# A softmax's reciprocal put first and its band product last in each DVE step, and the convolution's squares added earlier on POOL

## The chip, the cores and the metric

The kernel runs on one core of a Trainium2 chip. Its engines work in parallel, each through its own list of instructions in order, and meet at semaphores: TensorE (PE in the profile) multiplies matrices, VectorE (DVE) and ScalarE (ACT) work on vectors, GpSimd (POOL) too, and SyncE (SP) issues most DMAs. The metric is the device time of one execution in microseconds.

## The reference

A first transformer block is followed by two equal layers (sizes: 512 positions, width 1024, 16 query heads of 64 in 2 groups). The change lies in the two layers, in their attention and in the convolution beside it:

```python
# attention: each query block of 128 sees its own block and the one before, and a "sink"
s = jnp.einsum('bnqkgd,bnskd->bnkgqs', qb, kb) * scale
s = jnp.where(mask[None, :, None, None], s, -jnp.inf)
m = jnp.maximum(jnp.max(s, axis=-1, keepdims=True), sink)
p = jnp.exp(s - m)
p = p / (jnp.sum(p, axis=-1, keepdims=True) + jnp.exp(sink - m))
o = jnp.einsum('bnkgqs,bnskd->bnqkgd', p.astype(v.dtype), vb)
# convolution of 31 taps over the positions, then a layer norm over 512 channels
a = u * jax.nn.sigmoid(ug)
y = conv(a, w_dw) + b_dw
y = jax.nn.silu(layernorm(y, ln_g, ln_b))
c_out = jnp.einsum('btc,cd->btd', y, w_pw)
merged = jax.nn.sigmoid(ga) * a_out + jax.nn.sigmoid(gb) * c_out
x = x + jnp.einsum('btd,de->bte', merged, w_out[l])
```

## The kernel before

All large products are made in fp32 as three TensorE passes over split operands (L418, L419, L420: high by high, low by high, high by low), 512 columns each. Weights stream in units; ScalarE takes the high part, DVE the low part of each.

The attention of a layer is cut into 32 jobs (`LJ`), each a pair of heads on one block of 128 queries. A loop of 36 steps t is written out in the list of every engine, and the lists meet at semaphores (`A[...]`), which count jobs. What a job j passes through, and on which engine:

- TensorE, step j: scores, `scores` (L2140).
- DVE, step j, in `softmax`: a masked copy that packs the two key blocks into one (L2425; not in the last 8 jobs, of the first block), then for each head a custom instruction that adds the mask, scales and takes the maximum (L2441).
- ScalarE, step j: the exponential and its sum (L2287).
- DVE, step j+1, in `softmax`: the reciprocal of the sums (L2429).
- POOL, step j+1: the product with it, `scaled` (L2630), after a copy of the sink column for the job of that step (L2624).
- TensorE, step j+3: the transpose of the probabilities, `turn` (L2148). It writes a bank that the band product of the job before must have read: it waits for `A["banded"]` of job j-1.
- DVE, step j+3: the band product, `banded` (L2454), which puts the transposed probabilities apart for the two key blocks.
- TensorE, step j+4: the product with the values, `values` (L2161). DVE, step j+4: the gating, `gated` (L2463).

Between `turn` and `values` TensorE fills each step with chunks of other products, three passes each: the gates, and then the convolution's output product. How many is in the table `FILL_AT` (steps 4, 8, 11 and 13 have none, most have one to six). DVE has more work behind the gating in many steps: the gates' evictions (L2499, L2471), halves of weight splits (L796, L800), and the convolution's layer norm.

The layer norm's variance is made in the loop: DVE takes the mean off in steps 3 and 4, ScalarE squares, POOL adds the four squares to one in `sums_of_squares` (L2644), and TensorE sums over channels at the end of step 7 (`AT_SS`, L336). ScalarE takes the root (L2308), DVE inverts it in step 9 (L2517), and TensorE spreads it in step 13 (L343).

Of the kernel before, what the change touches and what calls it, by code (L numbers as in the profile page):

```python
# [101 lines left out]
def build(nc, w, x, mem, pos, pack, tables, cmask, w2, wg, rope2, out):  # L102
    ctx = ExitStack()
    with ctx:
        def sem(name):
            return ctx.enter_context(nc.semaphore(name))
# [1753 lines left out]
        def cross_dve(dve):  # L1860
# [92 lines left out]
            for j in range(11):  # L1953
# [14 lines left out]
        A = {n: sem("a_" + n) for n in ("scores", "packed", "max", "exp", "rec", "scaled", "turned",  # L1968
                                        "banded", "pv", "gated")}
        sink_in = sem("a_sink_in")  # L1970
        LJ = QB * 8
# [28 lines left out]
        def prob_at(j):  # L2000

            return j % 4

        def score_bank(j):

            return 2 if j % 2 == 0 else 0
# [5 lines left out]
        def block_of(j):  # L2012

            return (j // 8 + 1) % QB

        def query_factor(j, e=None):

            c = (j % 8 * QB + block_of(j)) * 2
            return rcol_head[:, c:c + 2] if e is None else rcol_head[:, c + e:c + e + 1]
# [4 lines left out]
        def asm(j, a_, e=None):  # L2024
            c = 16 * (j % 4) + a_
            return small[:, c:c + 2] if e is None else small[:, c + e:c + e + 1]
# [313 lines left out]
        def layer_dve(dve, L):  # L2340
# [76 lines left out]
            def softmax(j, o):  # L2417

                j, o = j if j < LJ else None, o if 0 <= o < LJ else None
                first = j is not None and block_of(j) == 0  # L2420
                if j is not None and not first:

                    pair = bank[:, score_bank(j):score_bank(j) + 2, :]
                    dve.wait_ge(A["scores"], (L * LJ + j + 1) * 2)
                    dve.copy_predicated(pair[:, :, P:2 * P], mask_b[:, P:2 * P].bitcast(U16).unsqueeze(1).to_broadcast([P, 2, P]),  # L2425
                                        pair[:, :, 0:P]).then_inc(A["packed"], 1)
                if o is not None:
                    dve.wait_ge(A["exp"], (L * LJ + o + 1) * 2)
                    dve.reciprocal(asm(o, 12), asm(o, 4)).then_inc(A["rec"], 1)  # L2429
                if j is not None:  # L2430
                    if j == 0:
                        dve.wait_ge(q_inv, L * 2 + 2)
                    if j >= 4:
                        dve.wait_ge(A["turned"], L * LJ + j - 3)
                    if not first:
                        dve.wait_ge(A["packed"], L * 24 + j + 1)
                    for e in range(2):
                        c = 2 * (j % 8) + e
                        if first:
                            dve.wait_ge(A["scores"], (L * LJ + j) * 2 + e + 1)  # L2440
                        dve.tensor_tensor_reduce(lprob[:, prob_at(j), e, 0:P], bank[:, score_bank(j) + e, P:2 * P],  # L2441
                                                 mask_b[:, P:2 * P] if first else mask_b[:, 0:P],
                                                 query_factor(j, e), neg_sink[:, L, c:c + 1], ALU.add, ALU.min, asm(j, 0, e)).then_inc(A["max"], 1)
# [34 lines left out]

            taps(FIRST_TAPS)
            for t in range(STEPS):  # L2480
                if 0 <= t - LAG_T < LJ:
                    banded(t - LAG_T)
                softmax(t, t - 1)
                if 0 <= t - LAG_V < LJ:
                    gated(t - LAG_V)
                if t == STEPS - 1:
                    dve.wait_ge(A["gated"], L * LJ + LJ)
                    dve.wait_ge(mg_sum, L * 8 + 7)
                    dve.wait_ge(co_ready, L * 8 + 8)
                    dve.tensor_tensor(sgb[:, 7, :], sgb[:, 7, :], sga[:, 7, :], ALU.add).then_inc(mg_sum, 1)  # L2490
                if t == 2:
                    roped(4)
                for f in FILL_END.get(t, ()):
                    if f < 6:
                        if f % 2:
                            dve.wait_ge(unit_done, L * V_N + base + V_FILL + f // 2 + 1)
                        else:
                            dve.wait_ge(fill_half, L * 3 + 6 + f // 2 + 1)
                        dve.tensor_tensor(sgb[:, 2 + f, :], bank[:, FILL_BANK[f], :], rbc[:, :], ALU.mult).then_inc(l_gs, 1)  # L2499
                    else:  # L2500
                        conv_gated(f - 6)
                if MERGE_LO_AT <= t:
                    merged_lo(t - MERGE_LO_AT)
                if t - 1 in L_SPLIT_AT:
                    n, p = L_SPLIT_AT[t - 1]
                    split_lo_part(dve, Unit(base + n, L), p, L * 6 + 6 + n - 16)
                if t < len(JOB_TAPS):
                    taps(JOB_TAPS[t])
                if t == AT_MEAN:
                    dve.wait_ge(ln_sum, L + 1)  # L2510
                    dve.tensor_scalar(acc[:, :], bank[:, 5, :], 1.0 / 512, None, ALU.mult).then_inc(ln_mu, 1)
                for m in CENTRE_AT.get(t, ()):
                    dve.wait_ge(ln_mu, L + 1)
                    dve.tensor_tensor(cy[:, m, :], cy[:, m, :], acc[:, :], ALU.subtract).then_inc(ln_c, 1)
                if t == AT_INV:
                    dve.wait_ge(cstd_ready, L + 1)
                    dve.reciprocal(rcol_ln[:, :], rcol_ln[:, :]).then_inc(cinv_ready, 1)  # L2517
                for m in NORM_AT.get(t, ()):
                    dve.wait_ge(crow_done, L + 2)
                    dve.wait_ge(ln_c, L * 4 + m + 1)  # L2520
                    dve.tensor_tensor(cy[:, m, :], cy[:, m, :], bank[:, 5, :], ALU.mult).then_inc(ln_n, 1)
                for m in LO_AT.get(t, ()):
                    dve.wait_ge(ln_hi, L * 4 + m + 1)
                    dve.tensor_tensor(c_lo[:, m, :], cy[:, m, :], c_hi[:, m, :], ALU.subtract).then_inc(ln_lo, 1)
# [61 lines left out]
        def _(pool):  # L2586
# [39 lines left out]
            def scaled(L, j):  # L2626
                row = lprob[:, prob_at(j), :, 0:P]
                pool.wait_ge(A["exp"], (L * LJ + j + 1) * 2)
                pool.wait_ge(A["rec"], L * LJ + j + 1)
                pool.tensor_tensor(row, row, asm(j, 12).unsqueeze(2).to_broadcast([P, 2, P]), ALU.mult).then_inc(A["scaled"], 1)  # L2630
# [6 lines left out]
            def sums_of_squares(L, which):  # L2637

                for n in which:
                    a_, b_ = ((0, 1), (2, 3), (0, 2))[n]  # L2640
                    pool.wait_ge(ln_sq, L * 4 + max(a_, b_) + 1)
                    if n == 2:
                        pool.wait_ge(ln_add, L * 3 + 2)
                    pool.tensor_tensor(conv_squares(a_), conv_squares(a_), conv_squares(b_), ALU.add).then_inc(ln_add, 1)  # L2644

            for L in range(LAYERS):
                pool.wait_ge(unit_done, L * V_N + U_L)
                pool.tensor_tensor(la[:, :, 0:PAD], ones_pad, ones_pad, ALU.subtract).then_inc(pad_ready, 1)
                pool.wait_ge(ident_in, TABLES_BEFORE + L * 16 + 16)
                for t in range(9):  # L2650
                    if t == 0:
                        pool.wait_ge(q_n, L + 1)
                    if t == 1:
                        pool.wait_ge(q_tabs, L * 2 + 1)
                    if t >= 2:
                        pool.wait_ge(q_rope, L * 9 + t - 1)
                    pool.tensor_tensor(lcos[:, t % 2, 0:T], lq[:, rope_at(t), :], cos_q[:, :] if t else cos2, ALU.mult).then_inc(q_cos, 1)
                for t in range(STEPS):
                    if t == 0:
                        pool.wait_ge(setup_step, SINKS_NEGATED)  # L2660
                        pool.wait_ge(q_ss, L * 9 + 9)
                    if t < LJ:
                        sink_column(L, t)
                    if t in (6, 7):
                        sums_of_squares(L, (0,) if t == 6 else (1, 2))
                    if 0 <= t - 1 < LJ:
                        scaled(L, t - 1)
                    if MERGE_HI_AT <= t:
                        merged(L, t - MERGE_HI_AT)
                for n in (1, 2) if L + 1 < LAYERS else (1,):  # L2670
                    sum_squares(pool, L * 2 + NORM_L + n)
# [125 lines left out]
```

## Time and profile before

| | us |
|---|---|
| three runs | 2242.09, 2242.54 (median), 2244.86 |
| profiled execution | 2238.4 |
| its span, first to last instruction | 2236.5 |
| TensorE busy | 2210.1 |
| DVE busy | 1284.1 |
| the loops, layer 0 and layer 1 | about 1026 to 1152 and 1716 to 1842 |

TensorE is almost never idle over the whole span, while DVE is busy for 57% of it. In the first part of each loop, though, DVE is busy nearly all the time. A row of the timeline gives start, length, engine, line, operation, output and inputs, the count of equal instructions merged, and in brackets the idle time of the engine before it with what ended it. DVE's instructions overlap: the next one starts some 0.1 us before the last has ended, so the time that one takes in a row of them is read from start to start.

### The profile page before, as it was taken

Reading aid. Unit: us, or ns where it says so; the run is one execution under the profiler, and the core shown is the slowest. Engines: PE = TensorE matmul, PEld = TensorE weight load, DVE = VectorE, ACT = ScalarE, POOL = GpSimd, SP = SyncE. Lnnn points to the kernel's source line nnn. Section 1 sums busy time; section 2 is a strip of 40 time slices with the busy share of each in tenths; the row PEclk is TensorE's granted clock in tenths of the full one; section 3 lists DMA queues with packets and bytes.
Section 4 is the critical chain, followed back from the end, with each engine's and each line's share of the span. In section 5 each row is a group of like instructions: output and inputs, shape, how many; then the busy total and the mean of one; then the engine's idle time right before and its main releaser. Section 6 shows DMA issues by size and latency. Waiting matters only on the chain.

```text
span 2236.5 us, 28991 instructions
## 1 busy us (share of the span) xinstructions
PE 2210.1 (99%) x11244; PEld 1805.3 (81%) x11244; DVE 1284.1 (57%) x1956; ACT 846.0 (38%) x1299; POOL 259.3 (12%) x281
## 2 busy tenths in 40 slices
PE   9999999999999999999999999999999999999999
PEld 7887788898888898886678888888887668888887
DVE  6468656445444226999874444332889874544422
ACT  5545454354333225223544333222322633433311
POOL 3000032120000001022231000011003232000000
PEclk9999999999999999999999999999999999999999
DMA  6221033123222222221122222223321122322222
GB/s 221 103 76 57 20 120 126 57 76 113 94 94 94 104 103 83 102 76 57 57 76 94 94 94 100 106 96 108 109 79 57 39 76 76 119 104 97 94 104 84
DMA packets 30484, 203.44 MB, mean 91 GB/s; under 512 B 3504, under 2 KB 4144, under 8 KB 6704
## 3 DMA queue, kind: packets, MB, share of 16 engines
q1 hardware_dynamic: 29088, 197.34, 24.7%
q10 hardware_dynamic: 1296, 4.72, 0.6%
q8 instruction: 68, 1.11, 0.2%
q14 instruction: 32, 0.26, 0.0%
HBM read 199.95 MB, written 2.10 MB: 90 GB/s over the span
## 4 chain that ended last, share of the span: by engine, by line
PE 87%; DVE 9%; issue 2%; ACT 1%; POOL 1%; DMA 0%; ACTq 0%; DVEq 0%; POOLq 0%
PE bank L418 25%; PE bank L420 25%; PE bank L419 25%; DVE cy L2361 3%; PE bank L2161 1%; PE bank L1005 1%; PE bank L2140 1%; DVE w_lo L304 1%; PE bank L2148 1%; PE bank L976 1%; POOL acc L327 1%; PE bank L2040 1%; PE bank L993 1%; DVE bank L2374 1%; PE bank L518 1%
## 5 line engine op out<-in xcount | busy, mean ns | idle before, releaser
L418 PE MATMUL bank<-x_hi,w_hi 128*128 128x512 f32 (+1 forms) x2032 | 789.9, 389 | 5.5 <-DVE x_lo L1777 2.3
L420 PE MATMUL bank<-x_hi,w_lo 128*128 128x512 f32 (+1 forms) x2032 | 775.0, 381 | 0.0
L419 PE MATMUL bank<-x_lo,w_hi 128*128 128x512 f32 (+1 forms) x2032 | 774.1, 381 | 0.0
L304 DVE TENSOR_TENSOR w_lo<-w_raw,w_hi 128x2048 fp32r<-128x2048 f32 x167 | 386.3, 2313 | 408.8 <-ACT w_hi L300 408.8
L300 ACT ACTIVATE w_hi<-w_raw 128x2048 fp32r<-128x2048 f32 x167 | 319.7, 1916 | 586.9 <-PE bank L420 585.0
L418 PEld LDWEIGHTS bank<-x_hi,w_hi 128*128 128x128 f32 x2032 | 382.1, 188 | 83.7 <-issue 6.6
L420 PEld LDWEIGHTS bank<-x_hi,w_lo 128*128 128x128 f32 x2032 | 381.9, 188 | 74.4
L419 PEld LDWEIGHTS bank<-x_lo,w_hi 128*128 128x128 f32 x2032 | 382.5, 188 | 72.7 <-issue 2.9
L418 PE MATMUL bank<-f_hi,w_hi 128*128 128x512 f32 (+1 forms) x572 | 213.3, 373 | 0.0
L419 PE MATMUL bank<-f_lo,w_hi 128*128 128x512 f32 (+1 forms) x572 | 213.2, 373 | 0.0
L420 PE MATMUL bank<-f_hi,w_lo 128*128 128x512 f32 (+1 forms) x572 | 213.2, 373 | 0.0
L2361 DVE SCALAR_TENSOR_TENSOR cy<-la,gains,cy 128x512 f32<-128x512 f32 x240 | 173.1, 797 | 0.0
L566 DVE TENSOR_TENSOR bank<-bank,rbc 128x512 f32<-128x512 f32 x66 | 46.0, 697 | 167.6 <-PE bank L420 159.6
L418 PEld LDWEIGHTS bank<-f_hi,w_hi 128*128 128x128 f32 x572 | 107.7, 188 | 19.1
L420 PEld LDWEIGHTS bank<-f_hi,w_lo 128*128 128x128 f32 x572 | 107.7, 188 | 19.0
L419 PEld LDWEIGHTS bank<-f_lo,w_hi 128*128 128x128 f32 x572 | 107.7, 188 | 18.6
L327 POOL TENSOR_TENSOR acc<-acc,sq 128x512 f32<-128x512 f32 (+1 forms) x48 | 80.6, 1680 | 142.0 <-ACT sq L311 138.3
L2287 ACT ACTIVATE lprob<-lprob,small 128x129 f32<-128x129 f32 x128 | 50.5, 396 | 101.9 <-DVE small L2441 101.9
L555 ACT ACTIVATE f_hi<-bank 128x512 f32 x66 | 39.5, 598 | 114.5 <-DVE bank L572 114.5
L574 DVE TENSOR_TENSOR f_lo<-bank,f_hi 128x512 f32 x66 | 45.7, 692 | 58.4 <-ACT f_hi L555 58.4
L327 POOL TENSOR_TENSOR acc<-sq 128x512 f32<-128x512 f32 (+1 forms) x8 | 14.4, 1800 | 442.8 <-ACT sq L311 442.8
L553 ACT ACTIVATE silu<-bank 128x512 f32<-128x512 f32 x66 | 38.8, 588 | 54.7 <-DVE bank L566 54.5
(360 smaller groups left out, 2624.0 us busy)
## 6 DMA issues: line engine op xcount, KB each, us to landing
w_raw<-w_d SPq DMA_DIRECT2D x184, 1024.0 KB, 4.8
out_d<-h SPq DMA_DIRECT2D x8, 256.0 KB, 6.5
h<-x_d ACTq DMA_DIRECT2D x3, 512.0 KB, 9.3
tab<-rope_d ACTq DMA_DIRECT2D x2, 768.0 KB, 4.2
memT<-mem_d ACTq DMA_DIRECT2D x1, 1024.0 KB, 4.8
w_raw<-w_d SPq DMA_DIRECT2D x2, 256.0 KB, 4.2
h<-x_d ACTq DMA_DIRECT2D x2, 256.0 KB, 5.9
w_raw<-w_d SPq DMA_DIRECT2D x1, 512.0 KB, 6.6
```

What stands on the lines that cost most here:

```text
L300: act.activation(w_hi[:, u.slot, :], w_raw[:, u.slot, :], ACT.Copy).then_inc(hi_ready, 1)
L304: dve.tensor_tensor(w_lo[:, u.slot, :], w_raw[:, u.slot, :], w_hi[:, u.slot, :], ALU.subtract).then_inc(lo_ready, 1)
L327: pool.tensor_tensor(acc[:, 0:width], sq[:, 0, 0:width] if k == 1 else acc[:, 0:width], sq[:, k % 2, 0:width], ALU.add).then_inc(acc_ready, 1)
L418: pe.matmul(dst, wh[:, k, cols], hi[:, kx_, at:at + width], start=start, stop=False)
L419: pe.matmul(dst, wh[:, k, cols], lo[:, kx_, at:at + width], start=False, stop=False)
L420: return pe.matmul(dst, wl[:, k, cols], hi[:, kx_, at:at + width], start=False, stop=stop)
L553: act.activation(silu[:, :], g, ACT.Silu).then_inc(silu_done, 1)
L555: act.activation(pick(f_hi, j, i), up, ACT.Copy).then_inc(f_hi_done, 1)
L566: dve.tensor_tensor(g, g, rbc[:, :], ALU.mult).then_inc(gu_scaled, 1)
L574: dve.tensor_tensor(pick(f_lo, j, i), up, pick(f_hi, j, i), ALU.subtract).then_inc(f_lo_done, 1)
L2287: act.activation(row, row, ACT.Exp, bias=asm(j, 0, e), scale=-1.0, accum_out=asm(j, 4, e)).then_inc(A["exp"], 1)
L2361: dve.scalar_tensor_tensor(out=cy[:, m, :], in0=src, scalar=wt, in1=cy[:, m, :], op0=ALU.mult, op1=ALU.add).then_inc(l_tap, 1)
```

## The change

DVE's `softmax` issues the reciprocal of the job before first, ahead of the masked copy of the new job, and the loop calls `softmax` ahead of `banded`. POOL adds the convolution's squares in steps 5 and 6 instead of 6 and 7, and behind `scaled` instead of ahead of it.

```diff
                 first = j is not None and block_of(j) == 0
+                if o is not None:
+                    dve.wait_ge(A["exp"], (L * LJ + o + 1) * 2)
+                    dve.reciprocal(asm(o, 12), asm(o, 4)).then_inc(A["rec"], 1)
                 if j is not None and not first:
                     pair = bank[:, score_bank(j):score_bank(j) + 2, :]
                     dve.wait_ge(A["scores"], (L * LJ + j + 1) * 2)
                     dve.copy_predicated(...).then_inc(A["packed"], 1)
-                if o is not None:
-                    dve.wait_ge(A["exp"], (L * LJ + o + 1) * 2)
-                    dve.reciprocal(asm(o, 12), asm(o, 4)).then_inc(A["rec"], 1)
...
             for t in range(STEPS):
+                softmax(t, t - 1)
                 if 0 <= t - LAG_T < LJ:
                     banded(t - LAG_T)
-                softmax(t, t - 1)
                 if 0 <= t - LAG_V < LJ:
                     gated(t - LAG_V)
...
                     if t < LJ:
                         sink_column(L, t)
-                    if t in (6, 7):
-                        sums_of_squares(L, (0,) if t == 6 else (1, 2))
                     if 0 <= t - 1 < LJ:
                         scaled(L, t - 1)
+                    if t in (5, 6):
+                        sums_of_squares(L, (0,) if t == 5 else (1, 2))
```

DVE's list of step 4 in layer 0 before (`lband` is the band product's output, `small` holds a job's maxima, sums and reciprocals, `lprob` its probabilities, `sga` its gated output):

```order
L2454 TENSOR_TENSOR lband<-bank,tab_133 128x512
L2425 COPY_PREDICATED bank<-mask_b,bank 128x2x128
L2429 RECIPROCAL small<-small 128x2
L2441 ISA lprob,small<-bank,mask_b,neg_sink,rcol_head 128x128
L2441 ISA small 128x1
L2441 ISA lprob,small<-bank,mask_b,neg_sink,rcol_head 128x128
L2441 ISA small 128x1
L2463 SCALAR_TENSOR_TENSOR sga<-sga,bank 128x128
L796 TENSOR_TENSOR w_lo<-w_raw,w_hi 128x1024
```

The same step in the changed kernel, with the head of step 5 behind it:

```order
L2423 RECIPROCAL small<-small 128x2
L2428 COPY_PREDICATED bank<-mask_b,bank 128x2x128
L2441 ISA lprob,small<-bank,mask_b,neg_sink,rcol_head 128x128
L2441 ISA small 128x1
L2441 ISA lprob,small<-bank,mask_b,neg_sink,rcol_head 128x128
L2441 ISA small 128x1
L2454 TENSOR_TENSOR lband<-bank,tab_133 128x512
L2463 SCALAR_TENSOR_TENSOR sga<-sga,bank 128x128
L796 TENSOR_TENSOR w_lo<-w_raw,w_hi 128x1024
L2514 TENSOR_TENSOR cy<-cy,acc 128x512 x2
L2423 RECIPROCAL small<-small 128x2
```

The reciprocal is the first instruction of the step, the band product stands behind the two maxima and ahead of the gating, and the reciprocal of the next step follows the layer norm's part. (The line numbers of the two moved instructions of `softmax` differ: 2423 and 2428 for 2429 and 2425.)

POOL's list in steps 5 to 7 of layer 0, as a difference:

```order
 L2630 TENSOR_TENSOR lprob<-lprob,small 128x2x128
+L2644 TENSOR_TENSOR la<-la 128x512
 L2624 COPY lprob<-neg_sink 128x2
-L2644 TENSOR_TENSOR la<-la 128x512
 L2630 TENSOR_TENSOR lprob<-lprob,small 128x2x128
+L2644 TENSOR_TENSOR la<-la 128x512 x2
 L2624 COPY lprob<-neg_sink 128x2
-L2644 TENSOR_TENSOR la<-la 128x512 x2
```

Each addition of squares (`la`) stands ahead of a sink copy that it stood behind, and behind the same product `scaled` (L2630) as before. The lists of TensorE, ScalarE and SyncE are the same.

## Rows read from the trace of the kernel before

**Rows 1.** The page's totals, TensorE's part of the line.
```profile
PE 2210.1 (99%) x11244; PEld 1805.3 (81%) x11244; DVE 1284.1 (57%) x1956; ACT 846.0 (38%) x1299; POOL 259.3 (12%) x281
```
**Rows 2.** TensorE's waits: total us, times, longest.
```profile
PE bank L336 <- POOL la L2644: 3.5, 2, 1.7
...
PE bank L2148 <- DVE lband L2454: 3.0, 4, 1.1
```
**Rows 3.** Timeline, layer 0, steps 6 and 7: POOL's additions, TensorE's sums behind them.
```profile
1053.54 3.31 POOL L2644 TENSOR_TENSOR la<-la 128x512 f32<-128x512 f32 x2
...
1056.89 1.05 PE L336 MATMUL bank<-ones,la 128*128 128x1 f32 x8 [1.73 <-POOL la L2644]
```
**Rows 4.** Timeline, layer 0, DVE in step 4.
```profile
1043.22 0.69 DVE L2454 TENSOR_TENSOR lband<-bank,tab 128x512 f32<-128x512 f32 x1
...
1043.82 0.42 DVE L2425 COPY_PREDICATED bank<-mask_b,bank 128x256 f32<-128x256 uint16 x1
...
1044.15 0.16 DVE L2429 RECIPROCAL small<-small 128x2 f32<-128x2 f32 x1
...
1044.39 0.41 DVE L2441 CUSTOM_DVE_ANT_0 lprob<-bank,mask_b,neg_sink 128x128 f32<-128x128 f32 x1
...
1045.06 0.29 DVE L2463 SCALAR_TENSOR_TENSOR sga<-sga,bank 128x128 f32<-128x128 f32 x1
```
**Rows 5.** Timeline, layer 0, DVE in steps 0 and 1.
```profile
1030.62 0.42 DVE L2425 COPY_PREDICATED bank<-mask_b,bank 128x256 f32<-128x256 uint16 x1
...
1031.20 0.41 DVE L2441 CUSTOM_DVE_ANT_0 lprob<-bank,mask_b,neg_sink 128x128 f32<-128x128 f32 x1 [0.15 <-DVE bank L2425]
...
1034.19 0.17 DVE L2429 RECIPROCAL small<-small 128x2 f32<-128x2 f32 x1
...
1034.32 0.41 DVE L2441 CUSTOM_DVE_ANT_0 lprob<-bank,mask_b,neg_sink 128x128 f32<-128x128 f32 x1
```
**Rows 6.** Timeline, layer 0, TensorE's transpose in step 5.
```profile
1044.05 0.41 PE L2148 MATMUL bank<-ident,lprob 128*128 128x128 f32 x2 [1.08 <-DVE lband L2454]
```
**Rows 7.** Timeline, layer 0, steps 8 to 12: DVE, and TensorE's transpose of step 12.
```profile
1059.67 0.69 DVE L2454 TENSOR_TENSOR lband<-bank,tab 128x512 f32<-128x512 f32 x1 [1.32 <-PE bank L2148]
...
1063.55 0.17 DVE L2429 RECIPROCAL small<-small 128x2 f32<-128x2 f32 x1 [0.42 <-ACT lprob L2287]
...
1064.76 0.29 DVE L2463 SCALAR_TENSOR_TENSOR sga<-sga,bank 128x128 f32<-128x128 f32 x1 [0.34 <-PE bank L2161]
...
1066.24 0.66 DVE L2454 TENSOR_TENSOR lband<-bank,tab 128x512 f32<-128x512 f32 x1
...
1069.85 0.44 PE L2148 MATMUL bank<-ident,lprob 128*128 128x128 f32 x2
```
**Rows 8.** Timeline, layer 0: DVE's steps 13, 19, 23, and the transposes one step later.
```profile
1074.00 0.69 DVE L2454 TENSOR_TENSOR lband<-bank,tab 128x512 f32<-128x512 f32 x1
...
1075.55 0.44 PE L2148 MATMUL bank<-ident,lprob 128*128 128x128 f32 x2
...
1100.09 0.69 DVE L2454 TENSOR_TENSOR lband<-bank,tab 128x512 f32<-128x512 f32 x1
...
1101.65 0.44 PE L2148 MATMUL bank<-ident,lprob 128*128 128x128 f32 x2
...
1111.93 0.69 DVE L2454 TENSOR_TENSOR lband<-bank,tab 128x512 f32<-128x512 f32 x1
...
1113.35 0.44 PE L2148 MATMUL bank<-ident,lprob 128*128 128x128 f32 x2
```
**Rows 9.** Timeline, layer 1: TensorE's transposes of steps 5 and 14.
```profile
1734.73 0.41 PE L2148 MATMUL bank<-ident,lprob 128*128 128x128 f32 x2 [1.08 <-DVE lband L2454]
...
1765.38 0.44 PE L2148 MATMUL bank<-ident,lprob 128*128 128x128 f32 x2
```
**Rows 10.** Stretches of 5 us: busy us of each engine, then granted clock, DMA share, GB/s.
```profile
1057.00:1062.00 5.00, 5.00 (x29) 3.17 (x30) 3.39 (x14) 3.09 (x7) 1.35 (x4) 0.66 0.01 3
1748.00:1753.00 5.00, 5.00 (x35) 3.54 (x34) 4.01 (x14) 4.07 (x9) 1.02 (x4) 1.00 0.02 3
```

## The prediction, made before the changed kernel was run

> **What bounds the kernel now.** I read the page's totals first, then TensorE's list of waits, then the timeline of the two attention loops (steps 0 to 35 of each layer). TensorE is busy in 99% of the span [rows 1], so only what makes TensorE stand still, or run at half clock, can move the time. Its waits that this change can touch are few: twice 1.7 us for POOL's sums of squares, and 3.0 us in four pieces, 1.1 the longest, for DVE's band product [rows 2]. The first is what the POOL part aims at; the second is a wait that the DVE part can lengthen. TensorE hardly waits in the loop because DVE delivers the band product early in each step, so I asked how much earlier than needed.
>
> **The change, part by part.** Nothing is added or removed; a DVE step and two places in POOL's list are put in another order.
>
> *POOL.* The squares move from step 6 to 5 and from 7 to 6, but also behind `scaled`. In POOL's list they therefore pass one sink copy and nothing else: each addition still follows the same `scaled`, which waits for the same reciprocal. The two late additions took 3.31 us and ended at 1056.85; TensorE's sums of squares waited 1.73 us for them [rows 3]. By itself the POOL part is worth the one copy at each place, a few tenths at most, and nothing below that bound except the sink copy behind 3.3 us of additions; the exponential that needs it comes later still. I take 0.
>
> *DVE: the length of a step.* Before, step 4 runs: band product at 1043.22, masked copy 0.60 later, reciprocal, first maximum at 1044.39, gating at 1045.06: 1.84 us [rows 4]. The reciprocal stood in the pause that the first maximum has behind the masked copy: with it there the maximum starts 0.57 after the copy [rows 4], without it 0.58 [rows 5]. So taking it out of there saves nothing, and in front it costs its own slot, 0.13 [rows 5]. A step grows to 1.97. In steps 1 to 3, which have one wait less in front of the maximum, reciprocal and copy together took 0.33 + 0.13 = 0.46 and will take 0.13 + 0.58 = 0.71: 0.25 each, 0.75 together.
>
> *DVE: the band product.* TensorE's transpose of job t-2 in step t+1 may start only when DVE's step t has done the band product of job t-3. That now starts 0.13 + 0.58 + 0.67 = 1.38 after DVE's step begins and takes 0.69; the transpose started 0.14 after it ended (1043.91, 1044.05) [rows 4, 6]. So the transpose is freed 2.21 us after DVE's step begins, where it was 0.83. Not shown in this trace is whether the maximum can start sooner when no reciprocal was just issued: its two bounds are 0.46 and 0.58, taken as 0.58 as in the only row of that kind. With 0.46 the 2.21 is 2.09. Now along the loop, where "late" is against layer 0 of the trace:
>
> - Step 4: DVE starts it at 1043.22 + 0.75 = 1043.97; the transpose that ran at 1044.05 runs at 1046.18, 2.13 late. Behind it in TensorE's queue stands everything: fill products, values, scores.
> - Step 7: TensorE reached the sums of squares at 1056.89 - 1.73 = 1055.16 and will reach them at 1055.16 + 2.2 = 1057.4, after POOL's 1056.9. The POOL wait is gone, eaten by the new one: 0.5 late.
> - Step 8: DVE comes 0.75 + 4 x 0.13 = 1.3 late, but had stood 1.32 for a transpose that waited behind those sums [rows 7]. The band product being last, that wait goes, and DVE starts step 8 as before, 1059.67. The reciprocal of job 8 came 3.88 later, at 1063.55, having waited for ScalarE, which waits for the maximum. The maximum now starts at 0.71 instead of 1.17, so the reciprocal comes at 1063.1, and now heads step 9.
> - Steps 9 to 11: step 9 is 1.97 plus what stood behind its gating (1064.76 to 1066.24, 1.48) [rows 7]: step 10 starts at 1066.55. Step 10 is 1.97 + 0.2 for gating: step 11 starts at 1068.7. Its band product frees the transpose of step 12 at 1070.9; it ran at 1069.85 [rows 7]: 1.05 late.
> - Step 13: DVE waits in step 12 for TensorE's values, so it comes equally late, 1074.00 + 1.05 = 1075.05; the transpose is freed at 1077.26 instead of 1075.55 [rows 8]: 1.7 late.
> - Steps 14 to 35: with three fill chunks or more in a step TensorE does not notice. Where the next step has one or two and DVE has a weight split or a gate behind its gating, it does: step 19 began at 1100.09 and frees at 1102.30 what ran at 1101.65, 0.65; step 23 at 1111.93 frees at 1114.14 what ran at 1113.35, 0.79, of which 0.25 are covered because DVE is by then less late than TensorE [rows 8]. There are five such places (16, 19, 20, 22, 23), about 2.1 us together, an estimate from these two and from the same subtraction at the others. After step 24 the masked copy falls away and the margin returns; at step 32 both wait for DVE's last gate, which is as late as TensorE.
>
> So 1.7 + 2.1 = 3.8 us in layer 0. In layer 1 the same step 13 came 0.85 us sooner relative to step 4 (1765.38 - 1734.73 against 1075.55 - 1044.05) [rows 8, 6, 9], because TensorE lost clock in layer 0 only: 0.66 granted in 1057 to 1062, 1.00 at the same place of layer 1 [rows 10]. The new path is set by DVE in both, so layer 1 loses 4.65. Sum 8.4 us: the profiled execution of 2238.4 (span 2236.5) would become 2246.8. The median of the runs shown, 2242.54, lies 4.1 above it; I carry the 8.4 over: **2250.9 us**. With 2.09 in place of 2.21 in the seven waits of a layer the sum is some 1.6 smaller: 2249.3.
>
> **The clock.** TensorE idles 1.73 us at the sums of squares in both layers; afterwards layer 0 ran at 0.66 of full clock, 1.2 and 2.4 GHz mixed, layer 1 at 1.00, which is 2.4 GHz [rows 3, 10]; so such a wait sometimes costs the full level. The Trainium skill (TensorE: Matmul & The Clock Gate, What's actually happening) says that half rate is the default and activity releases it, which speaks against a change that opens a longer idle stretch. The trace agrees in layer 0 and not in layer 1; by that rule the new stretch in step 5 would cost each layer what the second rival below gives.
>
> **The rivals.**
> 1. *Hidden after step 13.* The five late waits don't come, because DVE runs further ahead once it no longer waits for a transpose at the head of a step (TensorE's only long waits now stand in steps 5 and 7). Left is 1.7 + 2.55 = 4.2: 2246.7, within no change. Against it: at step 19 the margin was 0.73 and the delay is 1.38.
> 2. *Half clock at the new wait.* In step 5 TensorE stands from about 1043.9 to 1046.2, longer than the 1.73 that lost the clock in one layer of two. A stretch like that of rows 10 costs 5.00 x (1 - 0.66) = 1.7 us; in both layers 3.4 on top: 2254.3.
> 3. *Faster.* The reciprocal in front lets POOL scale and add sooner, the two POOL waits go (2 x 1.73) with layer 0's lost 0.85, and the band product is still in time: 2242.5 - 4.3 = 2238.2. It decides at step 5: if the band product of step 4 ends by the end of TensorE's scores, near 1043, this is what comes. For it speaks that the POOL wait is the longest touched; against it that DVE was already 1.08 us too late at just that place with the band product first [rows 6].
> 4. *The POOL part does nothing.* Its list passes only a copy; that is in the forecast and costs it nothing.
>
> **How the numbers follow.** Forecast 0.52, rival 2 0.22, rival 1 0.17, rival 3 0.09. A measurement of this kernel tells changes above 0.2%, 4.5 us, from none; slower by more than that are the forecast and rival 2, 0.74, within it rival 1, 0.17, faster rival 3, 0.09. The range reaches from 2243.5, which leaves out rival 3 and part of rival 1, to 2256, rival 2 with 1.7 us for a masked copy or weight split that collides with POOL's additions. The forecast's own range is 2248 to 2253.
>
> **What would show it.** TensorE's wait for the band product grows from 3.0 to 10 us or more, about 3 at step 5 of each layer, and appears at steps 12, 14, 20, 21 and 24; the wait for POOL's additions is gone; DVE's reciprocal opens each step, and DVE waits for ScalarE at step 9 longer than 0.42. It is wrong if the band product still ends before the scores of the next step, if steps 17 to 24 show no new wait, or if the sums of squares still wait for POOL.

## The result, and the profile after

The changed kernel takes 2244.86 us (median of 20 runs, 2243.05 to 2247.12), the kernel before 2241.45 us beside it (20 runs, 2238.77 to 2244.86). The ratio is 1.0015, 95% interval 1.0009 to 1.0021: 3.4 us slower. Slower was forecast, and 2244.86 lies in the range, but the forecast was 2250.9 and its step 8.4 us; less than half of that came. One run of experiment 6 below took 2635.81 us, at a mean granted clock of 0.781, and is left out of its numbers.

The profiled execution of the changed kernel took 2244.4 us, its span 2242.5, against 2238.4 and 2236.5: profile against profile it is 6.0 us. First the totals and TensorE's list of waits (total us, times, longest), which answer to [rows 1, 2]:

```profile
PE 2211.9 (99%) x11244; PEld 1806.2 (81%) x11244; DVE 1280.9 (57%) x1956; ACT 846.6 (38%) x1299; POOL 257.8 (11%) x281
```

```profile
PE bank L2148 <- DVE lband L2454: 11.2, 14, 2.2
PE bank L418 <- DVE w_lo L304: 2.7, 2, 1.6
...
PE bank L418 <- issue: 0.7, 2, 0.3
```

The wait for POOL's additions (3.5 us) is gone, and the wait for the band product has grown from 3.0 to 11.2 us, as forecast. Two lines were not foreseen: the wait at L418, TensorE's wait for the last gate in step 32, fell from 2.1 to 0.7, and a wait for a weight split (`w_lo`, L304) grew from 2.0 to 2.7, at 23 us into the run, where no instruction was moved. The first scores of layer 0 come 0.72 later than before (1027.48 for 1026.76), about as much as that wait has grown, so times within a loop are compared below from its first scores.

The timeline of step 4 and of the head of step 5, layer 0, after; it answers to [rows 4, 6]:

```profile
1043.93 0.16 DVE L2423 RECIPROCAL small<-small 128x2 f32<-128x2 f32 x1
1044.00 0.41 DVE L2428 COPY_PREDICATED bank<-mask_b,bank 128x256 f32<-128x256 uint16 x1
...
1044.56 0.41 DVE L2441 CUSTOM_DVE_ANT_0 lprob<-bank,mask_b,neg_sink 128x128 f32<-128x128 f32 x1
...
1045.22 0.69 DVE L2454 TENSOR_TENSOR lband<-bank,tab 128x512 f32<-128x512 f32 x1
...
1046.06 0.62 PE L2148 MATMUL bank<-ident,lprob 128*128 128x128 f32 x2 [2.19 <-DVE lband L2454]
1046.33 0.78 PE L418 MATMUL bank<-x_hi,w_hi 128*128 128x512 f32 x1
...
1049.97 0.39 PE L418 MATMUL bank<-x_hi,w_hi 128*128 128x512 f32 x1
```

The transpose starts 2.13 after DVE's step (2.21 was worked out): the reciprocal in front costs 0.07 from start to start, not 0.13. Behind the 2.19 us of standing still the fill products take 0.62 to 0.78 us each instead of 0.39; the first that takes 0.39 again starts at 1049.97. POOL, and the sums that wait for it, after [rows 3]:

```profile
1054.26 2.52 POOL L2644 TENSOR_TENSOR la<-la 128x512 f32<-128x512 f32 x2
...
1055.99 1.86 DVE L796 TENSOR_TENSOR w_lo<-w_raw,w_hi 128x1024 fp32r<-128x1024 f32 x1
...
1058.65 1.05 PE L336 MATMUL bank<-ones,la 128*128 128x1 f32 x8
```

The additions end at 1056.78, for 1056.85 before. From the first scores they start at the same place (26.78 us) and end 0.8 sooner, because they take 2.52 us instead of 3.31: DVE's weight split, which lay beside both of them, now starts during the second. The sums come 1.04 later than before by the same count and wait for nothing. The rest of the loop, by the transposes of layer 0 in steps 9, 12, 14, 20, 21 and 24, and the last gate in step 32 [rows 7, 8]:

```profile
1062.95 0.41 PE L2148 MATMUL bank<-ident,lprob 128*128 128x128 f32 x2 [1.03 <-DVE lband L2454]
...
1071.79 0.41 PE L2148 MATMUL bank<-ident,lprob 128*128 128x128 f32 x2 [0.55 <-DVE lband L2454]
...
1077.83 0.41 PE L2148 MATMUL bank<-ident,lprob 128*128 128x128 f32 x2 [0.32 <-DVE lband L2454]
...
1104.47 0.41 PE L2148 MATMUL bank<-ident,lprob 128*128 128x128 f32 x2 [0.50 <-DVE lband L2454]
...
1108.30 0.41 PE L2148 MATMUL bank<-ident,lprob 128*128 128x128 f32 x2
...
1116.89 0.41 PE L2148 MATMUL bank<-ident,lprob 128*128 128x128 f32 x2 [0.41 <-DVE lband L2454]
...
1138.58 0.41 PE L2148 MATMUL bank<-ident,lprob 128*128 128x128 f32 x2 [0.80 <-DVE lband L2454]
...
1139.33 0.47 PE L418 MATMUL bank<-o_hi,w_hi 128*128 128x512 f32 x1 [0.34 <-issue]
```

The same stretch of step 32 in the kernel before:

```profile
1134.67 0.41 PE L2148 MATMUL bank<-ident,lprob 128*128 128x128 f32 x2 [0.40 <-DVE lband L2454]
...
1136.14 0.47 PE L418 MATMUL bank<-o_hi,w_hi 128*128 128x512 f32 x1 [1.06 <-issue]
```

From its first scores (L2140) to DVE's last merge (L2490) the loop took 121.11 us in layer 0 and 120.20 in layer 1 before, 123.55 and 123.03 after: 2.44 and 2.83 more, 5.27 of the 6.0; the other 0.7 is the later start of the first loop. These loop lengths are the measure used below.

### The profile page after: what moved, and what is told of

It is laid out like the page before. It is cut to its first block, busy times and chain, and to the rows that moved or that the text cites. A ratio compares the mean times of both kernels' runs of the same rounds, so it can differ in the third digit from the quotient of the medians.

```text
span 2242.5 us, 28991 instructions
## 1 busy us (share of the span) xinstructions
PE 2211.9 (99%) x11244; PEld 1806.2 (81%) x11244; DVE 1280.9 (57%) x1956; ACT 846.6 (38%) x1299; POOL 257.8 (11%) x281
## 4 chain that ended last, share of the span: by engine, by line
PE 86%; DVE 10%; issue 2%; ACT 1%; POOL 1%; DMA 0%; ACTq 0%; DVEq 0%; POOLq 0%
PE bank L418 25%; PE bank L420 25%; PE bank L419 25%; DVE cy L2361 3%; PE bank L1005 1%; PE bank L2161 1%; DVE w_lo L304 1%; PE bank L2148 1%; PE bank L976 1%; POOL acc L327 1%; PE bank L2140 1%; PE bank L2040 1%; PE bank L993 1%; DVE lprob L2441 1%; DVE bank L2374 1%
## 5 line engine op out<-in xcount | busy, mean ns | idle before, releaser
L418 PE MATMUL bank<-x_hi,w_hi 128*128 128x512 f32 (+1 forms) x2032 | 791.5, 390 | 6.4 <-DVE w_lo L304 2.7
L304 DVE TENSOR_TENSOR w_lo<-w_raw,w_hi 128x2048 fp32r<-128x2048 f32 x167 | 386.3, 2314 | 408.5 <-ACT w_hi L300 408.5
L418 PEld LDWEIGHTS bank<-x_hi,w_hi 128*128 128x128 f32 x2032 | 383.0, 188 | 85.1 <-issue 6.7
L418 PE MATMUL bank<-f_hi,w_hi 128*128 128x512 f32 (+1 forms) x572 | 213.3, 373 | 0.0
L418 PEld LDWEIGHTS bank<-f_hi,w_hi 128*128 128x128 f32 x572 | 107.7, 188 | 19.0
L327 POOL TENSOR_TENSOR acc<-acc,sq 128x512 f32<-128x512 f32 (+1 forms) x48 | 78.7, 1640 | 141.6 <-ACT sq L311 137.9
L327 POOL TENSOR_TENSOR acc<-sq 128x512 f32<-128x512 f32 (+1 forms) x8 | 14.4, 1803 | 442.5 <-ACT sq L311 442.5
```

The costliest lines, as they stand in the source:

```text
L304: dve.tensor_tensor(w_lo[:, u.slot, :], w_raw[:, u.slot, :], w_hi[:, u.slot, :], ALU.subtract).then_inc(lo_ready, 1)
L327: pool.tensor_tensor(acc[:, 0:width], sq[:, 0, 0:width] if k == 1 else acc[:, 0:width], sq[:, k % 2, 0:width], ALU.add).then_inc(acc_ready, 1)
L418: pe.matmul(dst, wh[:, k, cols], hi[:, kx_, at:at + width], start=start, stop=False)
```

## The experiments

The theory: the loss is the band product standing last, through the transposes that wait for it, and the profile's difference is larger than the medians' because the profiled execution of before had lost little clock (TensorE had stood at half clock in few stretches). The rivals: that a wait in step 5 and the half clock behind it are the loss, or that POOL's additions or the reciprocal's place make it. Each kernel was timed in 11 runs, beside runs of the kernel before on the same chip: 33 of them (median 2242.35) for the first four kernels, 33 (2241.52) for the next four, and 27 (2241.68) for the last three.

**1. The kernel before again**, with no edit.

> The kernel before, unchanged. Theory A (the profiled execution of before was lucky: TensorE kept its clock in layer 1) expects a time within 0.1% of before, and in this second profile the granted clock below 0.8 in a stretch behind the sums of squares in both layers, with a profiled time of 2240 to 2242. Theory B (the profile was typical, the change's parts cancel each other) expects full clock in at least one layer again and a profiled time near 2238.4.

2241.47 us, ratio 0.9999 (0.9990 to 1.0008). What its profile shows matters more: the stretches behind the sums of squares in both loops (busy us of each engine, then the granted clock, DMA share, GB/s), which answer to [rows 10].

```profile
1060.00:1066.00 6.00, 6.00 (x34) 4.06 (x35) 4.02 (x16) 5.09 (x13) 1.48 (x4) 0.72 0.02 4
1750.00:1754.00 4.00, 4.00 (x22) 2.37 (x19) 2.33 (x10) 2.84 (x4) 0.74 (x2) 0.57 0.01 4
```

This execution lost clock in both layers, the one of [rows 10] in layer 0 alone, behind the same wait of 1.7 us; its loops took 121.10 and 121.05 us. The 93 runs of before that were timed beside the experiments, grouped by the mean granted clock of the whole run:

```
clock 0.999: 10 runs, median 2239.06 us
clock 0.998: 39 runs, median 2241.43 us
clock 0.997: 25 runs, median 2242.59 us
clock 0.996: 19 runs, median 2243.36 us
```

The profiled execution of before, 2238.4 us at 0.999, is like the 10. So 0.85 us by which layer 1 was "ahead" was luck of that execution, and a difference against it is too large. The mean clock counts more than the two loops, though. Experiment 1 lost clock at 316 to 320 us too, in the first block, where the kernel before, shown second, kept it:

```profile
316.00:320.00 4.00, 4.00 (x24) 4.00 (x23) 2.94 (x3) 1.58 (x1) 0.00 (x0) 0.59 0.43 180
316.00:320.00 4.00, 4.00 (x35) 4.00 (x35) 2.81 (x4) 1.99 (x2) 0.00 (x0) 1.00 0.52 217
```

**2. POOL's part alone.**

```diff
-                    if t in (6, 7):
-                        sums_of_squares(L, (0,) if t == 6 else (1, 2))
                     if 0 <= t - 1 < LJ:
                         scaled(L, t - 1)
+                    if t in (5, 6):
+                        sums_of_squares(L, (0,) if t == 5 else (1, 2))
```

> Only POOL's part: the squares behind the product of the step before, one sink copy earlier, DVE as before. Theory A expects no change, at most 0.4 us per layer faster (0 to -0.8 us), TensorE still waiting 1.5 to 1.7 us for POOL's additions in each layer. Theory B, in which this part gains and the band product loses, expects -2 to -4 us and the wait for POOL gone.

2240.64 us, ratio 0.9992 (0.9983 to 1.0001): no change that can be told. The median lies 1.7 under its neighbours, more than was expected, but that of the unedited kernel lay 0.9 under the same neighbours. The wait for POOL fell from 1.73 to 1.5 us, the copy that the additions passed.

**3. The reciprocal first, the band product where it was.**

```diff
+                if o is not None: ... dve.reciprocal(...)
                 if j is not None and not first: ... dve.copy_predicated(...)
-                if o is not None: ... dve.reciprocal(...)
```

> Only the reciprocal ahead of the masked copy; the band product stays first in the step, POOL as before. Theory A expects 0 to +1 us: a step of DVE grows by about 0.07 us, and the band product is as early as before. Theory B expects -2 us or more, since POOL scales earlier and its additions come earlier.

2240.14 us, ratio 0.9991 (0.9982 to 1.0000). It costs nothing; if anything it gains. By its median, 2.2 under the neighbours, theory B's number came and not theory A's, but at the edge of the noise. The wait for POOL falls to 1.2 us and does not go. Why the median should fall by more than that half microsecond per layer the profile doesn't show: its loop of layer 0 took 120.83 us, 0.3 less than before, and that of layer 1 122.41, at half clock for longer than any stretch of experiment 1 (0.57 from 1748 to 1756 us).

**4. The band product last, the reciprocal in its old place, POOL as before.**

```diff
             for t in range(STEPS):
+                softmax(t, t - 1)
                 if 0 <= t - LAG_T < LJ:
                     banded(t - LAG_T)
-                softmax(t, t - 1)
```

> Only the band product behind the maxima; the reciprocal between copy and maxima as before, POOL as before. Theory A expects nearly the whole change, +2.5 to +4 us, with TensorE's wait for the band product at 2.0 to 2.2 us in step 5 of each layer. Theory B expects +6 us or more.

2245.13 us, ratio 1.0011 (1.0002 to 1.0020): 2.8 of the 3.4 us. TensorE waits for the band product 11.4 us and no longer for POOL. So the loss is this part, and the POOL wait goes through it alone: from the first scores TensorE reaches the sums 2.3 us later (30.67 for 28.40), and POOL's additions end 0.8 sooner, as they do in the changed kernel.

**5 and 6. The whole change, but the band product last only in steps 0 to 8, or only from step 9.** The part of the edit that differs, against the kernel before:

```diff
+                if t < 9:            # in 6: t >= 9
+                    softmax(t, t - 1)
                 if 0 <= t - LAG_T < LJ:
                     banded(t - LAG_T)
-                softmax(t, t - 1)
+                if not t < 9:        # in 6: t >= 9
+                    softmax(t, t - 1)
```

> The whole change, but from step 9 on the band product is first in the step again. Theory A (the new wait in step 5 only takes the place of POOL's wait and its half-clock stretch; the loss is in the later waits of the loop) expects -1.5 to +1 us against before. Theory C (the loss is the 2.2 us wait in step 5 with the half clock behind it) expects +2.5 to +4 us, as the whole change.

> The whole change, but in steps 0 to 8 the band product is still first; from step 9 on it is last. Theory A expects +1.5 to +3.5 us, with TensorE's waits for the band product in steps 12 to 24 as in the whole change. Theory C expects -1.5 to +0.5 us.

Steps 0 to 8: 2240.75 us, ratio 0.9994 (0.9985 to 1.0003). From step 9: 2243.76 (ten runs), ratio 1.0009 (0.9999 to 1.0018), which touches no change; its two loops, at full clock, took 122.47 and 122.50 us, 2.3 more than the loop of before at full clock (120.20). So the 2.2 us of waiting in step 5, the longest new wait, cost nothing over the loop at full clock (120.17 us for 120.20) and 0.6 us where the clock was lost (121.73 for 121.10), since they replace the wait for POOL, and the short waits from step 9 on carry the loss. Number 5 also gives a price of the clock, since of its loops only that of layer 0 lost it. The stretches behind its wait in step 5, in both layers:

```profile
1048.00:1054.00 6.00, 4.75 (x16) 3.60 (x18) 5.39 (x16) 4.39 (x12) 1.95 (x5) 0.72 0.02 4
1738.00:1744.00 6.00, 3.80 (x24) 2.70 (x22) 5.71 (x17) 4.23 (x10) 1.59 (x4) 1.00 0.01 3
```

At 0.72 its loop took 121.73 us, at 1.00 120.17: 1.56 us.

**7. POOL's additions really sooner, DVE as before.** They stand in steps 5 and 6 and ahead of `scaled`, so that they need not wait for its reciprocal.

```diff
-                    if t in (6, 7):
-                        sums_of_squares(L, (0,) if t == 6 else (1, 2))
+                    if t in (5, 6):
+                        sums_of_squares(L, (0,) if t == 5 else (1, 2))
                     if 0 <= t - 1 < LJ:
                         scaled(L, t - 1)
```

> DVE as before; POOL adds the squares in steps 5 and 6, ahead of the product of the step, so that they no longer follow the reciprocal of that step. Theory A (half clock behind the wait at the sums is usual in the kernel before and costs 1 to 2 us a layer) expects the wait for POOL gone, full clock behind the sums and -3 to -6 us. The rival, that DVE sets steps 8 to 13 anyway, expects the wait gone and -0.5 to -2 us.

2237.72 us, ratio 0.9983 (0.9974 to 0.9992): 3.8 us faster than before, and by its median the fastest kernel of this study. Its timeline, layer 0:

```profile
1051.03 3.30 POOL L2644 TENSOR_TENSOR la<-la 128x512 f32<-128x512 f32 x2
...
1056.61 1.05 PE L336 MATMUL bank<-ones,la 128*128 128x1 f32 x8
```

The additions end 2.3 us before the sums, which wait for nothing, and no stretch of the two loops was granted less than the full clock. The loops took 119.54 and 119.50 us: 1.6 less than the 121.1 of experiment 1. That this is near the 1.73 of the wait is chance. Against the loop of before at full clock (120.20) it is 0.7, and the other 0.9 is the clock; of the wait, 0.84 us came back as a new one for the band product in step 6:

```profile
1049.94 0.41 PE L2148 MATMUL bank<-ident,lprob 128*128 128x128 f32 x2 [0.84 <-DVE lband L2454]
```

**8. Number 7 with the reciprocal first, and one fill chunk of step 5 moved to step 4** (`FILL_AT`: `4: 1, 5: 3` for `5: 4`).

> A version meant to be faster: the reciprocal first, the band product still first of all, POOL's additions ahead of the product in steps 5 and 6, and one chunk of fill products moved from step 5 to step 4, in front of TensorE's wait of 1.1 us. Theory A expects -4 to -7 us, with no stretch under 0.9 clock in the loops; the rival of e7 expects -1 to -3 us.

2238.28 us, ratio 0.9984 (0.9975 to 0.9993), loops 119.51 and 119.54. Neither edit adds anything to number 7, and the 4 to 7 us hoped for did not come.

**9. The changed kernel with two fill chunks of step 5 moved to step 4**, to fill the new wait.

```diff
-    ... 3: 1, 5: 4, ...
+    ... 3: 1, 4: 2, 5: 2, ...
```

> The changed kernel with two of the four chunks of fill products of step 5 moved to step 4, so that they lie in front of TensorE's 2.2 us wait for the band product. Theory A (that wait costs, net of POOL's wait that it replaces, only the half clock behind it) expects the wait at 0.9 us or less, full clock behind it and 243.5 to 245.5 us for the two loops together (246.6 in the changed kernel), so +0.5 to +2.5 us against before. Theory C expects the loss gone, -1 to +0.5.

2245.58 us, ratio 1.0015 (1.0006 to 1.0024), as slow as the changed kernel. The wait did not go; it moved by a step, as the transposes of steps 5 and 6 show:

```profile
1046.40 0.41 PE L2148 MATMUL bank<-ident,lprob 128*128 128x128 f32 x2 [0.81 <-DVE lband L2454]
1051.43 0.41 PE L2148 MATMUL bank<-ident,lprob 128*128 128x128 f32 x2 [2.01 <-DVE lband L2454]
```

Here DVE sets the pace, and TensorE's work only chooses where the wait stands. The profiled execution kept its full clock, with loops of 122.48 and 122.11 us, but only 3 of the 11 runs had a clock of 1.000 (median 2242.65); 7 had 0.998 (2245.64). So a full clock in the whole run, which was the point of this kernel, came in few of its runs: a miss. Where the others lost it no profile shows.

**10 and 11. Number 7 with the reciprocal first and the band product last only from step 9, or only from step 14.** The edit is that of 6 (`t >= 9`, `t >= 14`) on top of 7.

> Band product last from step 9 on only, reciprocal first everywhere, POOL's squares ahead of the product as in the faster version, so that neither the wait in step 5 nor the one for POOL is lengthened. Theory A expects each loop 2 to 2.6 us longer than in the faster version's 119.5, the time 0 to +1.5 us against before, with no stretch under 0.9 clock in the loops. The prediction's walk, which gave 3.8 us for these steps, expects 123 us a loop.

> As the run before, but the band product last from step 14 on only. The walk's late waits (steps 16, 19, 20, 22 and 23) come alone: by the walk 2.1 us a loop, by the trace of the changed kernel 1.25 less what step 32 gives back, so 0.8 to 1.3 us over 119.5, and the time -2.5 to -1 us against before.

From step 9: 2241.82 us, ratio 1.0002 (0.9993 to 1.0011), loops 122.00 and 121.90. From step 14: 2239.25, ratio 0.9988 (0.9979 to 0.9997), loops 120.32 and 120.30. None of the three lost clock in the loops of its profile, so the lengths can be subtracted: the band product last costs 2.4 us a loop from step 9 (against number 7), 0.8 of it from step 14 on, and so 1.6 to 1.7 in steps 9 to 13. The new waits of 11 in layer 0 are the changed kernel's from step 20 on: 0.50, 0.42 and 0.80 us at the transposes of steps 20, 24 and 32, and 0.34 for the last gate, where number 7 waits 1.06.

## Why the prediction was right and where it failed

**The mechanism was right.** The transpose freed 2.2 us into DVE's step, the POOL wait eaten by the new one, DVE waiting longer for ScalarE at step 9 (1.16 against 0.42), the POOL part passing only a copy: all came. Of the steps named for new waits, 12, 14, 20 and 24 have one, and 21 one too short for its row to show. A wait in step 9 was not named, and the one in step 32 grew from 0.40 to 0.80.

**One hit was luck.** The 0.75 that steps 1 to 3 were to cost did not come: from the first scores, DVE's step 4 begins at 16.45 us after and 16.46 before. The transpose of step 5 ran at 1046.06, close to the 1046.18 worked out, because the loop itself began 0.72 later; by the loop's own count it is 1.29 late and not 2.13. Little further hung on it, since the prediction let DVE's wait in step 8 take that delay back.

**Steps 9 to 13 were sized well.** The transpose of step 14 was to come 1.7 us late in layer 0. Counted from the first scores (1026.76 before, 1027.48 after) it came at 50.35 for 48.79: 1.56 late. In layer 1 it was 2.0 for the 2.55 forecast. Experiments 10 and 11 give 1.6 to 1.7 for these steps, but from number 7, which has no wait for POOL; that the figures agree is no check of this walk.

**The term that failed: "there are five such places (16, 19, 20, 22, 23), about 2.1 us together".** Between the transposes of steps 14 and 24 the delay against before grew from 1.56 to 2.82, by 1.26 instead of 2.1. The two places that the prediction works out (19 and 23) came nearly in full: 0.57 for 0.65 and 0.46 for 0.54, each short by the 0.08 by which the freeing was put too late. The three others, which hold the remaining 0.9, gave about 0.3: nothing at step 17, 0.19 at step 21 and 0.13 at step 23 (0.09 was given back in between). What was mis-sized there is the part that the prediction names at step 23 of DVE, the delay that is "covered because DVE is by then less late than TensorE". DVE's step 20 shows it, before and then after:

```profile
1103.86 0.69 DVE L2454 TENSOR_TENSOR lband<-bank,tab 128x512 f32<-128x512 f32 x1
...
1105.30 0.44 PE L2148 MATMUL bank<-ident,lprob 128*128 128x128 f32 x2
```

```profile
1106.17 0.15 DVE L2423 RECIPROCAL small<-small 128x2 f32<-128x2 f32 x1
...
1107.46 0.69 DVE L2454 TENSOR_TENSOR lband<-bank,tab 128x512 f32<-128x512 f32 x1
```

The prediction's subtraction would give 1103.86 + 2.21 - 1105.30 = 0.77 at this place. From the first scores DVE's step begins 1.59 late, while TensorE was already 2.10 late at the transpose of step 20 (1104.47 for 1101.65). The difference, 0.51, was covered; with the 0.08 of the freeing, 0.18 of the 0.77 is left. That little was lost: the transpose of step 21 starts 0.15 after the band product of 1107.46 has ended, which is the lag of a transpose that was waiting. At DVE's steps 16 and 22 the same cover was 0.23 and 0.18. Rival 1, in which none of the five comes, was nearer in the number (4.2) but not in kind, since two came.

Then the second half of the same step failed: "at step 32 both wait for DVE's last gate, which is as late as TensorE". There 0.72 came back, as the wait for that gate fell from 1.06 to 0.34 while the wait for the band product grew by 0.40 only. What is left of the 2.1 at the loop's end is 0.88 in layer 0 (2.44 - 1.56) and 0.85 in layer 1 (2.83 - 1.98); experiment 11 gives 0.8. That is 2.5 us of the 8.4, over two layers; the smaller delay of steps 9 to 13 is 0.7 more. Together they take the 8.4 down to about the 5.27 that the loops show.

**The carrying-over failed too.** "The median of the runs shown lies 4.1 above it; I carry the 8.4 over." The profile that served as the base was an execution of a kind that 10 of 93 runs show: it lost clock once, in layer 0. That of experiment 1 lost it three times, in both loops and at 316 us, and took 2.0 us longer, 0.85 of it in layer 1's loop and 1.1 ahead of the first scores. The changed kernel's profile lost it twice, in both loops, and lies 0.5 under the median of its runs, where that of before lies 3.05 under its own. So against that one profile the change is 6.0 us, against the profile of experiment 1 4.0, and between the medians 3.4. The change removes the POOL wait, behind which before loses clock, and opens another, behind which it loses clock itself; against a base that had lost it in one layer only, one of the two losses counts as the change's. Shown of the 2.6 us between 6.0 and 3.4 are the 0.85 in layer 1; how much of the rest lies in the loops and how much ahead of them no profile of a usual run of the changed kernel shows.

**Rival 2 came, as a substitute and not on top.** Half clock did follow the new wait, in both layers of the changed kernel. The stretches behind it, and the same place behind the sums [rows 10], where the clock is now whole:

```profile
1046.00:1050.00 4.00, 3.94 (x12) 3.21 (x13) 3.85 (x11) 2.65 (x6) 1.34 (x2) 0.57 0.02 6
1057.00:1062.00 5.00, 4.92 (x39) 3.17 (x37) 4.35 (x15) 2.48 (x7) 2.38 (x5) 1.00 0.12 49
1738.00:1744.00 6.00, 4.86 (x18) 3.81 (x20) 5.27 (x16) 4.48 (x12) 1.84 (x4) 0.72 0.01 3
```

A mean of 0.57 or 0.72 of full clock is a mix of the two levels, 1.2 and 2.4 GHz, after TensorE had stood 2.2 us for the band product. The rival priced it at 1.7 us a layer. In experiment 5, where one loop lost it and the other did not, it cost 1.56. In the changed kernel it costs about 1.1 and 0.9: the loops of experiment 9, at full clock, are that much shorter, though its fill chunks stand elsewhere too. That it costs less there because DVE sets the pace behind it fits, but was not tried. The Trainium skill (TensorE: Matmul & The Clock Gate, What's actually happening) has the half rate as the default that activity releases. The traces of the loops agree in kind: each loss there follows a wait of TensorE of 1.2 to 2.2 us. They also show that a wait of 1.7 or 2.2 us can pass without one (layer 1 of before, layer 1 of experiment 5), and the loss of experiment 1 at 316 us follows none: TensorE had not stood still since 296 us.

**Rival 3's idea was sound, in another kernel.** The two POOL waits and the clock were worth having: 2238.2 was worked out for it, and experiment 7 runs 2237.72, by putting the additions ahead of what waits for the reciprocal, and with the band product first. The nearness is chance in part, since the rival counted the two waits in full.

**What stays open.** Some of the loss lies ahead of the loops: the wait for the first weight split, at 23 us, is 0.7 us longer in the profiles of all seven kernels that have the band product last anywhere, and in none of the six that have it first, though no list differs before the loops. DVE and POOL take turns differently there: the last five input splits of DVE ahead of it (`x_lo`, L409) take 7.5 to 7.7 us in the seven and 6.5 to 6.6 in the six, the three additions of POOL (`acc`, L327) that follow take 6.3 and 8.2 to 8.5. What links this to the loops wasn't tried. The rest of the difference in when the loops begin is the clock: with no loss ahead of them the first scores come between 1026.4 and 1027.8 us (before, the changed kernel, 7, 8, 9), with one between 1027.9 and 1028.9 (1, 2, 3, 4, 6, 10), with two stretches or one of twice the length at 1030.2 and 1030.7 (11, 5). In the medians little of the 0.7 shows, since numbers 10 and 11 lie 4.1 and 1.5 us above number 7, and their loops alone are 4.9 and 1.6 longer. Also open is what decides, from run to run, whether a wait costs the clock.

## What to carry to other kernels

Within a step, the instruction that the busiest engine waits for stays ahead of those that only the slack engines wait for; what "one step sooner" is worth is read from the instruction that it stands behind, not from the step's number. Price a new wait only where the margin is clearly larger than the error of the step lengths it is made of, subtract at each such place what the earlier waits have already delayed, and follow a delay to the next place where the late engine had been waiting anyway, since there it is given back. Where one execution can lose clock and the next not, compare loops at the same clock, over several executions, before a difference against one profile is carried to a median.

## What the runs showed of the hardware

The same wait of 1.73 us cost the clock in both layers of one execution of the kernel before and in one layer of another; the loop with the full clock took 120.20 us, the others 121.05 to 121.11. The reciprocal on 128 x 2 takes 0.07 us of DVE's list where the masked copy behind it waits for nothing, less than half of the 0.16 that its row shows.

Two of POOL's additions take 3.3 us beside a weight split of DVE that starts 0.1 later, and the split 2.07, where one addition alone took 1.09 and the split alone 1.22 (first the split beside the additions, before, then each alone, after):

```profile
1053.64 2.07 DVE L796 TENSOR_TENSOR w_lo<-w_raw,w_hi 128x1024 fp32r<-128x1024 f32 x1
```

```profile
1046.02 1.22 DVE L796 TENSOR_TENSOR w_lo<-w_raw,w_hi 128x1024 fp32r<-128x1024 f32 x1
...
1049.23 1.09 POOL L2644 TENSOR_TENSOR la<-la 128x512 f32<-128x512 f32 x1
```

2 x 1.09 + 1.22 = 3.40, about the 3.31 that both together took [rows 3]: they ran one after the other. This is what the Trainium skill says (SBUF — State Buffer, SBUF: two separate sides): GpSimd and VectorE share a pair of ports under an exclusive lock, which an instruction of VectorE with two inputs in SBUF, as this split has, also takes, and the loser waits for the whole instruction. The trace agrees.
